# Reordering the TensorE units of one scan step by the shape of their products

## The reference, cut to what matters

```python
def step(S, inp):
    r_t, w_t, kk_t, akk_t, k_t, v_t = inp
    S = (S * w_t[:, :, None, :]
         - jnp.einsum('bhvk,bhk->bhv', S, kk_t)[..., None] * akk_t[:, :, None, :]
         + v_t[..., None] * k_t[:, :, None, :])
    return S, jnp.einsum('bhvk,bhk->bhv', S, r_t)
...
o = direction(0, lw_f, la_f, False) + direction(1, lw_b, la_b, True)
```

```python
q = (rms_norm(c_q, q_norm_w) @ w_uq).reshape(Bn, S, H_B, D_QK)
kv = (rms_norm(c_kv, kv_norm_w) @ w_ukv).reshape(Bn, S, H_B, D_NOPE + D_V)
...
q = apply_rope_tail(rms_norm(q, qk_q_norm_w))
k = apply_rope_tail(rms_norm(k, qk_k_norm_w))
```

## The kernel before

| unit | what | products, line | array shape | evicted by |
|---|---|---|---|---|
| U(s) | corrected values of chunk s, from the state | 24, L1537 | 64 x 64 | DVE L1416 |
| R(s) | what the state gives to the output | 24, L1537 | 64 x 64 | ACT L1325 |
| S(s) | new state | 24, L1545 | 128 x 64 | DVE L1428, L1431 |
| T(m) | transposes for the next step | 8, L1479 | 128 x 128 | ACT L1305 |
| A(m) | inner matrices of the next step | 32, L1489 | 64 x 64 | DVE L1404 |
| O | output of the step | 48, L1551 | 128 x 64 | DVE L1444 |
| C | transposed latents of the next step | 3, L1554 to L1556 | 128 x 128, one 128 x 64 | ACT L1335 |
| QK(n) | transposed queries or keys of the step before | 6, L1573 | 128 x 96 | ACT L1357 |
| KV, Y, XT | inner solve of the next step | 48 each for KV, the pair Y, the pair XT; L1509, L1496, L1502 | 64 x 64 | ACT, ACT, DVE |
| QKV(n) | queries, keys, values | L1565 to L1568 | 128 x 128 | ACT |
| U0, W1 | solve applied | L1517, L1524 | 64 x 64 | ACT |

## Time and profile before

### The profile page before, as it was taken

How to read it: one execution, slowest core, us unless ns; L and a number is a source line. 1 busy time by engine, 2 the same in 40 slices (tenths; PEclk the granted TensorE clock), 3 DMA queues, 4 the chain that set the end, 5 groups by cost and what they waited for, 6 DMA issues and landing times. The chain is left out here.

```text
span 5467.9 us, 94771 instructions
## 1 busy us (share of the span) xinstructions
PE 5195.8 (95%) x38844; PEld 2846.5 (52%) x38844; DVE 2824.3 (52%) x4438; ACT 2067.2 (38%) x3470; POOL 641.8 (12%) x1110
## 2 busy tenths in 40 slices
PE   8999999989989999989989999999899799999899
PEld 3444444478865555544444444444778655555454
DVE  2221486645545555556522214776455455555565
ACT  1211555345544444421112114553455444444211
POOL 0000000044430000001100000000445300000011
PEclk9999999999999999999999998999999999999999
DMA  5311565465541111036343115654656411110353
GB/s 225 140 67 56 182 214 193 142 169 148 159 122 48 25 42 31 6 116 221 118 160 140 70 55 181 214 193 144 169 144 165 120 45 25 43 31 6 107 174 117
DMA packets 570089, 646.07 MB, mean 118 GB/s; under 512 B 228336, under 2 KB 455152, under 8 KB 559872
## 3 DMA queue, kind: packets, MB, share of 16 engines
q1 hardware_dynamic: 569072, 638.88, 37.3%
q10 hardware_dynamic: 592, 1.15, 0.1%
HBM read 372.77 MB, written 267.13 MB: 117 GB/s over the span
## 5 line engine op out<-in xcount | busy, mean ns | idle before, releaser
L490 PE MATMUL ps<-feat_hT,w_features 128*128 128x512 f32 x2240 | 972.5, 592 | 0.0
L808 PE MATMUL ps<-w_tokens,prep_hT 128*128 128x512 f32 (+1 forms) x1920 | 826.9, 590 | 23.3 <-DMA prep_hT<-s_ht 23.3
L1701 PE MATMUL ps<-att_K,att_Q 96*128 96x512 f32 x1632 | 744.9, 599 | 31.9 <-DMA att_K<-s_qkt 22.2
L490 PEld LDWEIGHTS ps<-feat_hT,w_features 128*128 128x128 f32 x2240 | 420.4, 190 | 505.9 <-issue 502.8
L1813 DVE TENSOR_REDUCE att_mx<-ps 128x1 f32<-128x1024 f32 x384 | 470.3, 1225 | 291.0 <-PE ps L1701 291.0
L808 PEld LDWEIGHTS ps<-w_tokens,prep_hT 128*128 128x128 f32 x1920 | 365.8, 192 | 476.1 <-issue 450.1
L2094 PE MATMUL ps<-w_out,fin_yT 128*128 128x512 f32 x1280 | 569.5, 598 | 2.5 <-DVE fin_yT L2044 2.5
L1708 PEld LDWEIGHTS ps<-kc,att_pr 128*128 128x128 f32 x3264 | 367.4, 141 | 277.4 <-issue 231.5
L1777 ACT ACTIVATE att_PT<-ps 128x512 f32<-128x512 f32 x384 | 228.9, 596 | 642.1 <-PE ps L1708 641.3
L1701 PEld LDWEIGHTS ps<-att_K,att_Q 96*128 96x128 f32 x1632 | 297.3, 192 | 334.7 <-issue 276.2
L1768 ACT ACTIVATE att_pr<-ps,att_nb 128x1024 f32<-128x1024 f32 x384 | 424.4, 1110 | 80.2 <-DVE att_nb L1815 80.1
(11 more groups left out here) (226 smaller groups left out, 6794.8 us busy)
## 6 DMA issues: line engine op xcount, KB each, us to landing
s_sc<-prep_sc SPq DMA_DIRECT2D x20, 3072.0 KB, 9.2
scan_src<-s_sc SPq DMA_DIRECT2D x160, 384.0 KB, 4.9
s_qkt<-scan_qT SPq DMA_DIRECT2D x40, 576.0 KB, 4.1
fin_z<-s_zt SPq DMA_DIRECT2D x40, 576.0 KB, 5.2
s_zf<-feat_co SPq DMA_DIRECT2D x88, 256.0 KB, 2.5
s_ht<-feat_hT SPq DMA_DIRECT2D x10, 2048.0 KB, 7.9
prep_hT<-s_ht SPq DMA_DIRECT2D x40, 512.0 KB, 5.7
s_zt<-prep_st SPq DMA_DIRECT2D x80, 256.0 KB, 3.4
```

Of the source, the lines that this page charges most:

```text
L490: last = pe.matmul(b, wf[:, k, i * P:(i + 1) * P], hT[g % 2][:, k, :], start=(k == 0), stop=(k == KD - 1))
L808: last = pe.matmul(ps[:, tiles.bank(pieces[n]), 0:c1 - c0], hT[j % NH][:, k, :], wt[:, k, c0:c1], start=(k == 0), stop=(k == KD - 1))
L1701: pe.matmul(ps[:, c, :], Q[:, t * P:(t + 1) * P], K[:, k0:k0 + G], start=True, stop=True).then_inc(scored, 1)
```

## The change

Only the list that `step` returns is reordered. T(2) moves ahead of S(0), A(0) between S(0) and U(1), A(2) ahead of R(1), and both QK units behind O and C. No product, eviction or load is added or removed, and all conditions of waiting are derived anew from the list. Counting C as one shape and 96 columns as the full width, a step changed the array shape 15 times and now changes it ten times.

```diff
-        out = [("U", q, 0), ("R", q, 0)] + T[0] + T[1] + [("S", q, 0)] + T[2] + [("U", q, 1)] + A[0] + A[1]
-        out += [("R", q, 1)] + turn[0] + ([("S", q, 1)] if more else []) + A[2] + turn[1] + [("O", q)]
+        out = [("U", q, 0), ("R", q, 0)] + T[0] + T[1] + T[2] + [("S", q, 0)] + A[0] + [("U", q, 1)] + A[1] + A[2]
+        out += [("R", q, 1)] + ([("S", q, 1)] if more else []) + [("O", q)]
         if more:
-            out += [("C", nxt), ("KV", nxt)] + ys + xts + [("QKV", nxt, 0)] + applied(nxt) + [("QKV", nxt, 1)]
+            out += [("C", nxt)]
+        out += turn[0] + turn[1]
+        if more:
+            out += [("KV", nxt)] + ys + xts + [("QKV", nxt, 0)] + applied(nxt) + [("QKV", nxt, 1)]
         return out
```

## The result

The changed kernel takes **5518.18 us** (median of 4 runs, 5509.84 to 5523.24), the kernel before 5465.65 (4 runs, 5463.4 to 5469.98). The ratio is 1.0097, with a 95% interval of 1.0082 to 1.0112: 52.5 us slower. The forecast was 5491 with a range up to 5508. The direction was right, and the forecast increase of 23.6 was less than half of what came.

What follows compares the result with a forecast made beforehand. TensorE bounds the scan before; afterwards KV's wait for O's eviction does. Longer steps of 30.6 us, less 3 and 4, give 23.6: 5493.5 for the profiled execution, 5491 us as median, range 5464 to 5508.

Steps and rivals of the forecast that it cites:

- What bounds the step: In the scan, KV takes O's banks and waits 1.1 us for O's eviction, which VectorE reaches late behind head_sums and S(1).
- Its size: Each regular scan step, from U(0) to KV, becomes 0.72 us longer: 13.99 against 13.27.
- The first step: Each layer's first step with a KV has no QK, so it loses 1.6 us more, 2.3 in all.
- 30.6: Sum of the longer scan steps over two layers, 2 x 15.3 us, before anything is taken off.
- The deductions: Taken off the sum: 3 us for O's vanished waits for QK(0), 4 us for issue gaps hidden in KV's wait.
- TensorE as the bound: Rival: TensorE's own order still sets the scan step, 0.37 to 0.52 us shorter; 5448 to 5454 us, chance 0.11.
- every removed change of shape counts: Rival: all five removed shape changes a step save 0.14 us each, 27 us in all; 5441 us, chance 0.02.
- No measurable change: Rival: all of TensorE's about 25 us of issue gaps go into the wait at KV; 5470 us, chance 0.10.
- slower still: Rival: late squares, masks or loads bind, nothing hides, 0.3 us a step comes on top; 5509 us, chance 0.07.

Runs made afterwards that it cites:

- before_kv_on_o: The kernel before in its old order, with only KV's banks changed to O's pair; 5502.80 us, 1.0084 of before.
- with small loads: The kernel before and the changed kernel, each with the scan's row loads cut to a twelfth of their bytes from the fourth tile on; 5432.02 and 5480.83 us.
- padded kernels: The kernel before and the changed kernel, each with 128 already fulfilled waits on TensorE ahead of the first layer's scan; 5473.84 and 5515.64 us.
- store kernels: The kernel before and the changed kernel, with the output stored ahead of the keys (5489.37, 5509.02 us) or behind the next loads (5469.92, 5529.01 us).
- sums_and_masks: The changed kernel with head_sums behind O's eviction on VectorE and GpSimd's masks ahead of latent_roots; 5453.75 us, 0.9984 of before.

## Why the prediction was right and wrong

*What bounds the step (right).* The bound moves from TensorE to the chain R(1), squares, head_sums, S(1), O, KV. The trace of after shows every link in the order forecast, but at its start A(2)'s eviction is as late as the squares (6.68 and 6.66 after S(0)), so that VectorE's queue alone would do. The short wait of head_sums for the squares that was forecast is not there. Three kernels bear out what follows head_sums: adding the one hand-over to the old order costs 0.83 a step, removing it from the new one gives 0.97 back, and moving head_sums out of the queue gives 1.1 back.

*Its size (nearly right).* 0.72 a regular step was forecast, 0.89 measured. VectorE's S unit, taken as 1.12 from start to start, takes 1.49 the second time (1611.12 to 1612.61), because it meets GpSimd's masks, which puts O's start at 9.44 instead of 9.08. KV then follows the eviction's end by 0.10 instead of 0.25. That meeting stood in my own numbers (S(1)'s second operation from 8.55 after S(0), the masks from 8.75), and I hadn't laid the two engines side by side.

*The first step (wrong, small).* I added 1.6 for the step that has no QK. The hand-over there is another: KV gets a pair that is free, and Y waits for ACT instead, so that this step grows by 0.82 and 1.13 in the two layers (with small loads). The steady hand-overs were worked through and used for a step that is not in the steady state. Over two layers it is some 2.7 us less than forecast. Terms so far: 38 x 0.89 = 34 (with this step counted as a regular one) where I had 30.6.

*The deductions (the failed step).* The forecast took 4 us off for issue gaps that "fall between S(1) and KV" and "hide in the new wait", and 3 because O no longer waits for QK(0). The first of these is the term that failed. Measured, the issue gaps don't shrink by 4 but grow, from 26 to between 37 and 49 in the kernels with this order and these waits. before_kv_on_o shows that the wait alone hides none (26.4 for 26.2). A gap is TensorE's instructions arriving late behind data (26 to 1.8 when the row loads are cut). The padded kernels suggest that it counts which instructions a late fetch carries, and a new order shuffles this anew. I had held the gaps of before as a constant of the stage. O's waits (3.9) are gone indeed, but C waits 2.8 us for the rotation tables in their place, so that about 1 us was won where 3 had been taken off.

*The sum as it came.* 34 for the undisturbed steps and 8 to 19 for the rest, against 30.6 and -7. In the profiled execution the 38 steps are 46.5 longer. The rest of that execution is 6.6 shorter than before's, and it lies 8.3 below its own median.

*What stays open.* Why the new order has more gaps than the old was not settled. Padding moved the gaps of the profiled executions by 10 us down and 9 up, but the distance of the medians by only 6 to 11, and the waits' own cost is not known. The kernels with small traffic show that few gaps are left without it (4 and 1.8), and the store kernels that moving the stores brings none of the added gaps back. How much of the added gaps another padding would take away, and whether some of it belongs to this order in any place, no run tells.

*The rivals.* TensorE as the bound (5448 to 5454) is refuted for this change. Once VectorE's queue, the masks and the load are taken out of the way, a kernel with this order does reach this and more, 5430 (the earlier load was not tried without the new order). That every removed change of shape counts is refuted too: four of five fall between R(1) and KV, and their 0.63 shows up only there. No measurable change would have needed all gaps in the wait. The case "slower still" at 5509 came nearest in size, but for another reason: neither late squares nor masks bound, the gaps grew. The range ended below what came.

*The rule of the Trainium skill* ("TensorEngine Tiling (Array Packing)", section Key Properties) says that a change of mode drains TensorE. The trace of sums_and_masks, where TensorE is the bound, agrees that a change costs time, 0.16 each. In the changed kernel it is worth nothing.

## What to carry to other kernels

When an order is changed, work through who gets whose PSUM bank afterwards, and for each hand-over on the critical engine ask when the former user's eviction ends. An eviction that nobody waited for can cost 0.83 us a step from one hand-over alone. When the bound engine is saved some work, look for what ends next in line, in turn: here O's eviction, the masks, a load. The changed order with the first moved was 17 us slower than the old kernel, with two moved 9 faster, with all three 31 faster. And don't carry issue gaps over as a constant: traffic that is hidden as data holds up the fetching of instructions, and the orders tried here had from 17 to 42 us of such gaps with the same work.

## What the runs showed of the hardware

- TensorE's instructions come on a DMA queue of their own and stand behind data. With the loads of rows cut, 26 us of issue gaps become 1.8; with the stores of the changed order cut, 42 become 26, and with stores and loads cut 4. With 128 idle waits ahead of the scan the two longest gaps were gone in one profiled execution, and a new one of 3.0 was there in another.
- VectorE with two operands from SBUF, or with a copy from SBUF to SBUF, and GpSimd slow each other down: 0.98 instead of 0.56 us for L1434, 0.53 instead of 0.25 for the copy, 2.41 instead of 2.11 for the masks. Before, it was GpSimd that lost: L1247 began 0.05 after L1431 of S(1) and took 0.60, where its like now takes 0.22. L1447, which reads PSUM, keeps its 1.01.

```profile
1586.55 0.60 POOL L1247 TENSOR_SCALAR scan_ss<-scan_ss 128x2 f32<-128x2 f32 x1 [7.18 <-ACT scan_csq L1290]
```

- A change of the array's shape costs about 0.16 us here (0.63 for four).
